# A two-layer mixer trunk on one core: a gate product, a modulation block, the first state's blocks, two high parts, a table load and four fills stand elsewhere in their engines' orders

## The reference

```
h = rmsnorm(x, norm1_g[l]) * (1 + sc1) + sh1          # sc1, sh1, ... from c @ w_mod
z = h @ w_cat                                          # gates and the inputs of three mixers
ya = rglru_branch(...); yb = diff_attention(...); yc = rwkv7_mix(...)
merged = (sigmoid(z[..., 0:D]) * (ya @ w_merge_a) + sigmoid(z[..., D:2*D]) * (yb @ w_merge_b)
          + sigmoid(z[..., 2*D:3*D]) * (yc @ w_merge_c))
x = x + gt1 * (merged @ w_out)
...
# inside rwkv7_mix, per head: S_t = S_{t-1} diag(w_t) + (S_{t-1} a_t) b_t^T + v_t k_t^T; o_t = S_t r_t
```

## Time and profile before

| | |
|---|---|
| median of 3 runs | 1070.72 us (1070.26 to 1072.43) |
| the profiled execution's own time | 1072.69 us |
| its span in the profile | 1070.9 us |
| mean granted TensorE clock | 0.994 |
| TensorE busy | 1048.0 us (98%) |
| VectorE busy | 849.9 us (79%) |
| ScalarE busy | 587.2 us (55%) |
| GpSimd busy | 115.6 us (11%) |

### The profile page before, as it was taken

One profiled execution on the slowest core, in us unless ns is written; L12 is line 12 of the kernel. 1 busy time (PEld: TensorE's weight loads), 2 busy tenths in 40 slices (PEclk: granted clock), 3 DMA queues, 4 the chain that ended last, 5 costly groups with the idle time before them and its releaser, 6 DMA issues.

```text
span 1070.9 us, 24039 instructions
## 1 busy us (share of the span) xinstructions
PE 1048.0 (98%) x9982; PEld 961.1 (90%) x9982; DVE 849.9 (79%) x1272; ACT 587.2 (55%) x913; POOL 115.6 (11%) x138
## 2 busy tenths in 40 slices
PE   7999999999999999999999999999999999999997
PEld 6789988787789999999989999778877999999997
DVE  5698999686686898986779899968766788888763
ACT  2266567632465766663365575783328476666433
POOL 0100000055101000001120000002530100000001
PEclk9999999999999999999999999999999999999999
DMA  9955545544246766667865546451615565545651
GB/s 366 356 191 210 185 169 219 212 157 142 100 158 215 259 240 217 240 243 266 317 209 200 197 162 235 164 202 63 231 62 196 194 240 197 188 172 188 235 199 40
DMA packets 42088, 215.07 MB, mean 201 GB/s; under 512 B 8336, under 2 KB 8976, under 8 KB 22672
## 3 DMA queue, kind: packets, MB, share of 16 engines
q1 hardware_dynamic: 30480, 171.85, 43.9%
q0 software_dynamic: 11520, 41.95, 11.2%
HBM read 212.21 MB, written 1.05 MB: 199 GB/s over the span
## 4 chain that ended last, share of the span: by engine, by line
PE 83%; DVE 7%; DMA 7%; SPq 1%; ACT 1%; issue 1%; DVEq 0%; ACTq 0%
PE ps L1852 16%; PE ps L1853 16%; PE ps L1854 16%; PE ps L2066 6%; PE ps L2070 6%; PE ps L2064 6%; DMA mring<-wmod_dram 5%; PE ps L1872 4%; DVE macc L1144 2%; PE ps L2173 2%; DMA TK<-wmod_dram 2%; PE ps L1890 1%; PE ps L1816 1%; PE ps L2164 1%; PE ps L2021 1%
## 5 line engine op out<-in xcount | busy, mean ns | idle before, releaser
L995 ACT ACTIVATE WH<-ring 128x1024 fp32r<-128x1024 f32 x140 | 147.8, 1059 | 156.7 <-PE ps L1854 153.3
L1688 DVE TENSOR_TENSOR WLO<-ring,WH 128x1024 fp32r<-128x1024 f32 x140 | 169.2, 1222 | 58.0 <-ACT WH L995 57.9
L1853 PE MATMUL ps<-HL,WH 128*128 128x256 f32 x736 | 206.1, 280 | 0.0
L1854 PE MATMUL ps<-HH,WLO 128*128 128x256 f32 x736 | 206.1, 280 | 0.0
L1852 PE MATMUL ps<-HH,WH 128*128 128x256 f32 x736 | 205.0, 279 | 0.0
L1852 PEld LDWEIGHTS ps<-HH,WH 128*128 128x128 f32 x736 | 139.1, 189 | 0.1
L1853 PEld LDWEIGHTS ps<-HL,WH 128*128 128x128 f32 x736 | 137.6, 187 | 0.1
L1854 PEld LDWEIGHTS ps<-HH,WLO 128*128 128x128 f32 x736 | 137.6, 187 | 0.0
L578 POOL DMA_DIRECT2D mring<-wmod_dram x80 | 43.2, 540 | 751.3 <-DVE macc L1144 446.8
L1144 DVE SCALAR_TENSOR_TENSOR macc<-mring,sm,macc 128x1024 f32<-128x1024 f32 x70 | 96.5, 1378 | 17.0 <-DMA mring<-wmod_dram 14.7
L1852 PE MATMUL ps<-GH,WH 128*128 128x256 f32 x384 | 108.5, 282 | 0.4 <-DVE WLO L1688 0.4
(11 more groups left out here) (409 smaller groups left out, 2492.7 us busy)
## 6 DMA issues: line engine op xcount, KB each, us to landing
ring<-wmain_dram SPq DMA_DIRECT2D x150, 1024.0 KB, 5.0
mring<-wmod_dram POOLq DMA_DIRECT2D x80, 512.0 KB, 4.8
G<-wmod_dram SPq DMA_DIRECT2D x3, 1024.0 KB, 9.2
R<-wmod_dram SPq DMA_DIRECT2D x2, 1024.0 KB, 18.4
TK<-wmod_dram SPq DMA_DIRECT2D x2, 1024.0 KB, 20.0
X<-x_t_dram SPq DMA_DIRECT2D x1, 1024.0 KB, 5.1
R<-wmod_dram SPq DMA_DIRECT2D x2, 512.0 KB, 12.2
y_dram<-H SPq DMA_DIRECT2D x4, 256.0 KB, 2.2
```

What stands on the lines that cost most here:

```text
L995: A(WH[:, n % 2, part], ring[:, b, part], ACT.Copy).then_inc(hi_ready, 1)
L1688: V.tensor_tensor(WLO[:, n % 2, part], ring[:, b, part], WH[:, n % 2, part].bitcast(F32), ALU.subtract).then_inc(lo_ready, 1)
L1853: MM(out, w_high[:, at], low, start=False, stop=False, skip_group_check=True)
L1854: return MM(out, w_low[:, at], high, start=False, stop=stop, skip_group_check=True)
```

## The change

Six edits, each in both layers:

1. ScalarE makes high parts 8 and 9 ahead of both Gelu reads, instead of between them.
2. ScalarE loads the table set for Ln (`LOGARITHM`) right behind `gate_out(2)`; before, the load stood at the first Ln.
3. VectorE makes low parts 8 and 9 right behind L1351, ahead of two products that it did first before.
4. VectorE does `gated(2)` behind the last "m" mask instead of behind the fourth level's transposes, and the modulation block that followed it there stands ahead of `gated(3)`.
5. For c = 0 the two blocks of `ST` are made straight from the sum times the decay, and the compact copy `STC` after them; before, `STC` came first and the blocks were copies of it. Three counts of `st_ready` are given, and one wait on each of VectorE and TensorE is added for c = 1.
6. TensorE issues four fills ahead of the third `chunk_products`.

```diff
@@ ScalarE, input projection
+                half_pairs_high(8, 10)
                 for k in (LR + 2, LR + 3):
                     evac(l, k, YA[:, 2 * (k - LR) - 4:2 * (k - LR) - 2, :], ACT.Gelu_apprx_tanh)
-                    half_pairs_high(2 * (k - LR) + 4, 2 * (k - LR) + 6)
+                half_pairs_high(10, 12)
@@ ScalarE, attention's end
                 gate_out(2)
+                act.preload_act_table_set(LOGARITHM)
                 act_chunks(14, 16)
@@ VectorE, input projection
                 V.tensor_tensor(KK[:, :, :], KK[:, :, :], E[:, :, :], ALU.mult).then_inc(kk_used, 1)
+                half_pairs_low(8, 10)
                 V.tensor_tensor(LRA, CUM, LD, ALU.subtract).then_inc(cm_ready, 1)
                 dve.wait_ge(kk_used, l + 1)
                 V.tensor_tensor(AB[:, :, :], AB[:, :, :], KK[:, :, :], ALU.mult).then_inc(step, tick(n_step))
-                half_pairs_low(8, 10)
@@ VectorE, solve
                         elif par == 1 and v < 4:
                             mod_beside(1)
+                        elif par == 1:
+                            gated(2)
...
-                            if v == 3:
-                                gated(2)
-                            mod_beside(1)
+                            if v < 3:
+                                mod_beside(1)
...
                     V.tensor_tensor(dst, oct(4 + n), over(small_mask(M_UPI), 8), ALU.mult).then_inc(rb_ev, 1)
+                mod_beside(1)
                 gated(3)
@@ VectorE, chain of states
                             dve.wait_ge(st_zero, l + 1)
-                            V.tensor_tensor(STC, added_, decay, ALU.mult).then_inc(step, tick(n_step))
-                            after()
                             for half, block in blocks_:
-                                V.tensor_copy(block, STC[half]).then_inc(st_ready, 1)
+                                V.tensor_tensor(block, added_[half], decay[half], ALU.mult).then_inc(st_ready, 1)
+                            V.tensor_tensor(STC, added_, decay, ALU.mult).then_inc(st_ready, 1)
                         else:
+                            if c == 1:
+                                dve.wait_ge(st_ready, 7 * l + 3)
@@ TensorE, solve
                 chunk_products(6, KK, AB, t_mm)
+                fill_some(4)
                 pe.wait_ge(t_ev, base + 2)
                 chunk_products(4, AB, KK, t_mm)
@@ TensorE, chain of states
                     if c < NCH - 1:
+                        if c == 1:
+                            pe.wait_ge(st_ready, 7 * l + 3)
```

More of the change, by code:

```diff
@@ L1606, in _ @@
                             if c < NCH - 2:
-                                dve.wait_ge(st_ready, 6 * l + 2 * c + 2)
+                                dve.wait_ge(st_ready, 7 * l + 2 * c + 3)
                                 V.tensor_tensor(STC, STC, decay, ALU.mult).then_inc(step, tick(n_step))
@@ L2251, in _ @@
                     if c:
-                        pe.wait_ge(st_ready, 6 * l + 2 * c)
+                        pe.wait_ge(st_ready, 7 * l + 2 * c + (1 if c > 1 else 0))
                         for j in range(4):
@@ L2284, in _ @@
                     pe.wait_ge(gn_sq, 2 * (l + 1))
-                    pe.wait_ge(st_ready, 6 * (l + 1))
+                    pe.wait_ge(st_ready, 7 * (l + 1))
                     pe.wait_ge(u_ready, 3 * (l + 1))
```

## The result

The changed kernel takes 1089.75 us, median of four runs (1088.43 to 1091.20), against 1070.75 for the kernel before (1070.26 to 1072.43) in the same session: a ratio of 1.0178, with a 95% interval of 1.0165 to 1.0190. I had forecast 1072.3 and a range up to 1074.8. The profiled execution took 1089.85, its span is 1088.0, 17.1 more than before. The profile before was itself about 1.5 us late when it reached the places of the change in layer 0 (TensorE starts L2121 at 187.49, the same products in the changed kernel at 186.00; four other profiles with the code of before up to there are 1.2 to 1.6 earlier than it too), so 17.1 understates the loss; the medians differ by 19.0.

The account below looks back on a forecast made before the run. TensorE, busy 1048.0 of 1070.9 us, was taken as the bound, so only its waits count. Terms gave +0.57 in layer 0 and +1.06 in layer 1, together +1.6 on 1070.72: 1072.3 us, range 1069.6 to 1074.8.

Parts of the forecast that it names:

- Table load: Attention's end: the earlier load delays the squares by 1.25 us, removes the 0.38 wait at L1816; +0.9 per layer.
- rival of a dearer load: At the added table load: a drain of its own costs 1.3 more per layer, total 1074.9 us; chance 0.08.
- Four fills: Ahead of the third product: fills use TensorE's 0.53 us wait and save 0.92 after the mixing; -0.7 per layer.
- gated(2) and block out of the solve: Solve's last level: the mask no longer waits behind them; gain 1.14 us in layer 0, 0.65 in layer 1.
- What the block drags with it: First state: GpSimd's issue waits for the moved block, delaying low part 26 and zeroing; +1.26 us per layer.
- Behind the blocks: After ST's blocks: STC, a low part and L1589 make TensorE wait; +0.25 us per layer, bounds 0 and 1.4.
- a rival of 0.10: First state onward: GpSimd's late sums stretch VectorE's chain, +1.4 per layer, total 1075.1 us; chance 0.10.
- High and low parts: Parts 8 and 9, layer 1: the 1.10 us wait at 624.57 goes, 1.0 comes near 641; net 0.
- GpSimd is in time: First state: zeroing does not wait for the moved block, waits vanish; total 1068.5 us; chance 0.10.

Follow-up runs that it names:

- Without the load: Changed kernel with the modulation block ahead of the read masks and the added table load undone: 1068.31 us, ratio 0.9984.
- the issue behind low part 26: Changed kernel with GpSimd's modulation transfer issued one step later, after low part 26 and ahead of the zeroing of ST: 1084.35 us, ratio 1.0120.
- the run with one wait: Changed kernel with one GpSimd wait ahead of its first sum, for its own zeroing of ST: 1077.86 us, ratio 1.0075.
- block back: Changed kernel with the modulation block again in the solve, ahead of the last level's mask: 1070.77 us, ratio 0.9994.
- issue behind: Changed kernel with the transfer that waits for the moved block issued after GpSimd's six sums: 1070.72 us, ratio 1.0005.
- block ahead of the masks: Changed kernel with the modulation block ahead of the read masks instead of after them: 1069.96 us, ratio 0.9996.
- more fills: Changed kernel with ten more fills on TensorE ahead of the wait for the first WY: 1085.32 us, ratio 1.0139.
- halves: Changed kernel with STC made in two instructions, so VectorE asks for low part 27 later: 1086.40 us, ratio 1.0150.
- memsets: Changed kernel with a one-column GpSimd memset ahead of each of its sums but the first: 1087.05 us, ratio 1.0154.
- block moved alone: Kernel before with only the modulation block moved, to stand after the read masks: 1091.72 us, ratio 1.0192.
- issue late: Kernel before with GpSimd waiting for the read masks before issuing the modulation transfer; low part 26, zeroing and six sums follow: 1093.26 us, ratio 1.0187.
- sums late: Kernel before with GpSimd zeroing ST and making its six sums only after VectorE's four read masks: 1070.97 us, ratio 1.0007.
- low part 26 late: Kernel before with GpSimd making low part 26 only after the read masks, the transfer's issue staying early: 1073.16 us, ratio 1.0024.
- a wait each: Changed kernel with a GpSimd wait ahead of each sum but the first, for the end of its sum before: 1078.75 us, ratio 1.0083.
- the sums behind the chain: Changed kernel with GpSimd's six sums waiting until VectorE has made the chain's last WY: 1097.01 us, ratio 1.0248.

## Why the prediction was wrong

- **Table load (+0.9 per layer): right.** The wait for the squares is 1.10 where I had 1.25, and the one of 0.38 ahead of L1816 is gone. No drain shows around the added load, and the wait is shorter than the load itself (1.28), so the rival of a dearer load is out. Without the load the kernel was 1.65 us faster in the same session, where 1.8 was due; the intervals of the two overlap.
- **Four fills (-0.7): right at its place, wrong in the sum.** The wait of 0.53 is gone, and the product behind comes 4.1 us behind the first `chunk_products` in place of 3.8, 0.3 later where I had 0.22. The stops of 0.8 to 1.5 us at L2169 that come with the fills were in none of my rivals; at 0.8 to 2.8 us over both layers they take back from half of the term's 1.4 to twice it.
- **gated(2) and block out of the solve (-1.14, -0.65): right**, by TensorE's rows. In layer 1 a wait of 1.16 came at an earlier level of L2178, behind a block whose own transfer was late (VectorE stood 3.36 us for it); of the other profiles only that of the issue behind low part 26 has such a one (1.38, in layer 0).
- **What the block drags with it (+1.26): right.** From the start of the read masks to the first state it is 269.26 - 260.81 = 8.45 us, where I had 8.43. The issue waits for the block, low part 26, the zeroing and the first state follow (the wait at L2260 is 1.84 and 1.91; I had 1.9), and with the issue taken from there all of it is gone.
- **Behind the blocks (+0.25, upper bound 1.4): this step failed.** It measured +7.4. I had seen that the six sums now start with the first state, and gave this mechanism a rival of 0.10; what I got wrong is its price. I read "2.17 beside L622 and 1.18 alone" as a stretch by 1.8. The same rows say something else: low part 27 ends at 269.52 + 2.17 = 271.69, and GpSimd's last sum at 268.02 + 2.59 = 270.61, 1.1 before it. It had stood still for 1.0 and then run at full speed. With a factor the cost is bounded by the work's own length, with exclusion only by the length of GpSimd's run, here 7.4 us of sums. But exclusion from one sum at a time costs only 1.8 per layer (18.6 less 16.8, the run with one wait), near the rival's 1.4. What makes 7.4 of it are two costs that neither the term nor the rival had: with GpSimd's issue ahead of the sums VectorE is let in at none of the four boundaries behind the sum in which it asks, and the clock falls behind TensorE's idle time, which costs about as much again as the wait of 3.34 (an estimate, above). The two together are 12 us of the total by the run with one wait.
- **High and low parts (0): right.** The wait of 1.10 at 624.57 is gone, one of 1.04 stands at 647.82, 6.0 behind the 641.82 of before; this kernel is 7.14 - 0.92 = 6.2 late since the norm and the four fills.
- *GpSimd is in time*, my rival of 1068.5, is what three kernels made true (block back, issue behind, block ahead of the masks): 1069.96 to 1070.77. They are 1.5 to 2.3 us slower than that rival; the stops at L2169, 0.8 to 2.8 us in their profiles, can be that, and no run splits it.

The Trainium skill (SBUF — State Buffer, Who interferes with whom) says that a VectorE instruction with two SBUF inputs contends with a GpSimd instruction that reads SBUF, and that whoever issues first has the shared pair for the whole instruction. By that, low part 27 would have waited for one sum: the run with one wait added shows this (2.30 us, 1077.86). The changed kernel shows more than the Trainium skill has, a whole run of sums passed over it (7.06 us, 1089.75), and the measurement decides.

## What to carry to other kernels

Where two instructions on VectorE and GpSimd overlap and one is long, look at whether the long one ends when the other ends plus its own length. Then it stood still, as low part 27 did here, and the price goes by the other engine's run, not by a factor. When an edit delays an engine, list what then runs back to back on it, who is held by that run, and what the tensor engine's clock does in the idle time. A semaphore wait of GpSimd for its own last instruction, between a transfer it issues and a run of sums, cost 0.12 us here and gave 12 back; moving the issue behind the run gave back all.

## What the hardware did that I had not expected

- Seven kernels had GpSimd issue a transfer and then run up to and through the six sums without a gap (changed, more fills, halves, memsets, block moved alone, issue late, issue second). In both layers of all seven VectorE's instruction (a sum of two SBUF operands, or a copy within SBUF) stood still to the end of the run, 6.5 to 7.25 us. In the others, with six sums in a row behind a wait (sums late, low part 26 late, one wait, a wait each), it got its turn at the next boundary. Taking the issue out or putting one wait behind it changes the one into the other. What in the issue does it is open.
- While VectorE has its turn GpSimd's next sum is longer by about 1 us (3.50 for two in place of 2.49), so part of the loss changes sides.
- The clock was at the lower level in part of the 5 us windows (0.63, 0.54) behind idle times of 1.8 to 3.3 us of TensorE. A wait of 1.9 us at the first state took it to 0.50 in layer 1 of the run with the sums behind the chain, and the same wait left it at 1.00 in the run with one wait. So not every idle time of this length costs clock; what decides is open.
- TensorE stops for 0.8 to 1.5 us inside a row of small products when the four added fills stand ahead of them in its program; the profile names no engine for it. A packet of the instruction queue begins 2.2 to 2.5 us before TensorE goes on, in every stop listed.
